# Three layers' modulation rows: from TensorE in the recurrence and attentions to GpSimd products and ScalarE row sums in projection and feed-forward

## The reference, cut to what matters

```
# first block (a bidirectional gated delta rule, then a convolved gated feed-forward)
mod  = silu(c)  @ w_mod[0] + b_mod[0]          # 6 x 1024; shift1, scale1 are needed at once
h    = rms(x) * (1 + scale1) + shift1;  x = x + gate1 * mixer(h)
h    = rms(x) * (1 + scale2) + shift2;  x = x + gate2 * ffn(h)
# layer 2.0 (sliding-window attention + gated linear attention), layer 2.1 (causal attention)
mod2 = silu(c_2) @ ada_w[layer] + ada_b[layer] # 6 x 1024 for each of the two layers
...  x = x + gate1 * mixer(h);  x = x + gate2 * mixture_of_experts(h)
```

## Time and profile before

| what | value |
|---|---|
| median of three runs (lowest, highest) | 2882.66 us (2880.57, 2885.34) |
| the profiled execution, first to last instruction (its span) | 2876.6 us, 6.1 below the median |
| mean granted TensorE clock | 0.970 of full speed |
| `gdn_project` | 41.4 to 320 us; a round from round 2 to 3 takes 14.1 us |
| `gdn_prepare`, `gdn_core` | 320 to 334.7, 334.7 to 739.9 us |
| `gdn_finish` | 739.9 to 820.6 us; TensorE's last seven tiles 766 to 815 |
| `ffn` | 820.6 to 1244.6 us; an input round 12.1 us; output tiles from 1103 |
| `even_attention` | 1378 to 1459 us |
| `causal` | 2221 to 2298.6 us |

### The profile page before, as it was taken

How to read it: one execution, slowest core, us unless ns; L and a number is a source line. 1 busy time by engine, 2 the same in 40 slices (tenths; PEclk the granted TensorE clock), 3 DMA queues, 4 the chain that set the end, 5 groups by cost and what they waited for, 6 DMA issues and landing times. The chain is left out here.

```text
span 2876.6 us, 36427 instructions
## 1 busy us (share of the span) xinstructions
PE 2668.0 (93%) x13974; PEld 1723.2 (60%) x13974; DVE 1433.5 (50%) x2832; ACT 630.3 (22%) x1348; POOL 157.4 (5%) x179
## 2 busy tenths in 40 slices
PE   6999899999999999979998699999799998899998
PEld 4888778889568888858654233333587544333332
DVE  4767566677356675466524132234554623233334
ACT  3132355556411110012332000000213421000000
POOL 0000222222000000000100000000000000000000
PEclk8999999999999999999999899999999999899999
DMA  6111555420222222222547999999422558999998
GB/s 267 59 49 69 173 171 171 147 89 16 88 73 88 87 84 86 88 68 74 191 165 280 417 418 417 418 418 418 153 79 77 159 199 337 418 417 418 417 418 353
DMA packets 112694, 613.86 MB, mean 213 GB/s; under 512 B 12976, under 2 KB 13440, under 8 KB 62720
## 3 DMA queue, kind: packets, MB, share of 16 engines
q1 hardware_dynamic: 102240, 576.68, 52.2%
q0 software_dynamic: 8832, 30.44, 3.0%
q10 hardware_dynamic: 1440, 4.29, 0.4%
HBM read 602.85 MB, written 8.51 MB: 213 GB/s over the span
## 5 line engine op out<-in xcount | busy, mean ns | idle before, releaser
L3099 PE MATMUL bank<-arena 128*32 128x512 f32 (+2 forms) x2048 | 407.0, 613 | 39.2 <-DMA arena<-in_w 30.9
L470 PE MATMUL bank<-arena 128*128 128x256 f32 x1776 | 409.7, 384 | 20.3 <-ACT arena L438 13.9
L470 PEld LDWEIGHTS bank<-arena 128*128 128x128 f32 x1776 | 338.3, 192 | 88.8 <-issue 33.7
L3099 PEld LDWEIGHTS bank<-arena 128*32 128x32 f32 (+2 forms) x2048 | 137.7, 132 | 284.8 <-issue 279.1
L3127 PE MATMUL bank<-arena 128*32 128x512 f32 (+2 forms) x1024 | 210.8, 636 | 37.1 <-DMA arena<-in_w 34.8
L3141 PE MATMUL bank<-arena 128*128 128x512 f32 x448 | 219.6, 614 | 5.5 <-DVE arena L3260 1.8
L259 PE MATMUL bank<-arena 128*128 128x512 f32 (+1 forms) x608 | 210.0, 502 | 0.9 <-PEq L2546 0.9
L3274 DVE SCALAR_TENSOR_TENSOR arena<-bank,arena 128x512 f32<-128x512 f32 x224 | 168.3, 751 | 74.0 <-PE bank L3141 62.0
L3127 PEld LDWEIGHTS bank<-arena 128*32 128x32 f32 (+2 forms) x1024 | 69.5, 136 | 173.6 <-issue 168.9
L259 PEld LDWEIGHTS bank<-arena 128*128 128x128 f32 x608 | 114.9, 189 | 92.5 <-issue 85.4
L3141 PEld LDWEIGHTS bank<-arena 128*128 128x128 f32 x448 | 71.3, 188 | 151.7 <-DVE arena L3274 90.0
(11 more groups left out here) (492 smaller groups left out, 3957.2 us busy)
## 6 DMA issues: line engine op xcount, KB each, us to landing
arena<-in_w SPq DMA_DIRECT2D x384, 1024.0 KB, 20.1
arena<-in_dense SPq DMA_DIRECT2D x308, 512.0 KB, 4.3
arena<-core_rows POOLq DMA_DIRECT2D x48, 256.0 KB, 5.6
arena<-in_xT SPq DMA_DIRECT2D x2, 2048.0 KB, 12.5
token_rows<-arena ACTq DMA_DIRECT2D x8, 512.0 KB, 5.4
gdn_gate<-arena POOLq DMA_DIRECT2D x8, 256.0 KB, 2.7
arena<-gdn_gate SPq DMA_DIRECT2D x1, 2048.0 KB, 7.8
arena<-band_bias POOLq DMA_DIRECT2D x2, 1024.0 KB, 6.1
```

What stands on the lines that cost most here:

```text
L470: mm = pe.matmul(out, w[:, k, :], x[:, k, :], start=(k == 0), stop=(k == K1 - 1))
L3099: mm = pe.matmul(self.bank[2 + t][part, :], xT[i % 2][:, 2 * q + k, part], w[j][:, k, t, :], start=(q == 0 and k == 0), stop=(q == 3 and k ...
```

## The change

The 128 weight columns' tiles are no longer in `dense`. They are in an input of their own, `mods`, laid out with the output column on partitions and the 1024 weights along the row. A result is then a sum along the row of weight times condition. GpSimd multiplies a tile in place by the row `silu(c)` (for n below 32) or `silu(c_2)`, which stands on all partitions (`mod_scale`), ScalarE copies the tile onto itself and accumulates into the one column `mod_all[:, 16+n]` (`mod_sum`), and then, where told, waits for that sum and issues the load of a later tile into the slot. VectorE adds the bias for many columns at once. 32 tiles are handled in `gdn_project`, 20 in `gdn_finish`, 76 in `ffn`; three, eight, eight and four slots serve them. Nothing is left in `gdn_core`, `even_attention` and `causal`. The second condition row is activated once and stored in DRAM (`c2_dram`), and read back twice.

```diff
+    def mod_load(self, eng, n):
+        eng.dma_start(self.mod_slot(n), self.ins["mods"][n]).then_inc(self.mod_loaded[self.mod_place(n)[1]], 16)
+    def mod_scale(self, pool, n):
+        pool.wait_ge(self.mod_loaded[self.mod_place(n)[1]], 16 * self.mod_nth[n])
+        pool.tensor_tensor(self.mod_slot(n), self.mod_slot(n), self.mod_row(n), ALU.mult).then_inc(self.mod_scaled, 1)
+    def mod_sum(self, act, n, more=None):
+        act.wait_ge(self.mod_scaled, n + 1)
+        act.activation(self.mod_slot(n), self.mod_slot(n), ACT.Copy, accum_out=self.mod_all[:, 16 + n:17 + n]).then_inc(self.mod_summed, 1)
+        if more is not None:
+            act.wait_ge(self.mod_summed, n + 1)
+            self.mod_load(act, more)
...
 # gdn_project, ScalarE
+                def mods(i, q):
+                    n = 4 * (i - 1) + q
+                    if 0 <= n < 32:
+                        self.mod_sum(act, n, n + 3 if n + 3 < 32 else None)
+                act.dma_start(c_row, self.ins["c_rows"][0]).then_inc(self.mod_row_loaded, 16)
+                act.dma_start(c2_row, self.ins["c_rows"][1]).then_inc(self.mod_row_loaded, 16)
+                self.mod_load(act, 1)
+                self.mod_load(act, 2)
                 self.shift_steps(act, jobs, scaled, ready)
+                act.wait_ge(self.mod_row_loaded, 32)
+                act.activation(c2_row, c2_row, ACT.Silu).then_inc(c_silu, 1)
+                act.activation(c_row, c_row, ACT.Silu).then_inc(c_silu, 1)
+                act.wait_ge(c_silu, 1)
+                act.dma_start(self.c2_dram[:, :], c2_row).then_inc(c2_stored, 16)
                 for i in range(12):
+                    mods(i, 0)
+                    if i == 0:
+                        act.wait_ge(c2_stored, 16)
+                        self.mod_load(act, 0)
...
 # gdn_core, TensorE
-                    if p < groups:
-                        pieces += [(mod_rows, k, 0) for k in range(sum(steps[:l]), sum(steps[:l + 1]))]
...
 # gdn_finish
                 sp.dma_start(gate, self.gate_dram.rearrange("p (h t) -> p h t", h=H)).then_inc(gate_in, 16)
+                sp.dma_start(self.mod_row(32), self.c2_dram[:, :]).then_inc(self.mod_row_loaded, 16)
+                for n in range(32, 40):
+                    self.mod_load(sp, n)
...
+                def mods(m):
+                    for n in range(32 + 3 * m, min(35 + 3 * m, 52)):
+                        self.mod_sum(act, n, n + 8)
...
 # ffn: GpSimd, ScalarE's input loop, ScalarE's output loop, VectorE's end
+            @block.gpsimd
+            def _(pool):
+                for n in range(52, 100):
+                    self.mod_scale(pool, n)
+                pool.wait_ge(self.mod_row_loaded, 64)
+                for n in range(100, NMODS):
+                    self.mod_scale(pool, n)
...
+                    if m < J + 1:
+                        for n in range(52 + 4 * m, 56 + 4 * m):
+                            self.mod_sum(act, n, n + 8 if n + 8 < 100 else None)
...
+                for n in range(100, 104):
+                    self.mod_load(act, n)
                 for k in range(KD):
+                    if k % 2 == 0:
+                        for n in range(100 + 7 * k // 2, 107 + 7 * k // 2):
+                            self.mod_sum(act, n, n + 4 if n + 4 < NMODS else None)
...
+                self.mod_keep(dve, 32, NMODS)
```

More of the change, by code:

```diff
@@ L271, in row_product @@
         return mm
[L274 to L293, removed]
-                                 bank[:, 256:264].rearrange("p (n q) -> p q n", q=4),
-                                 self.S("mod_b", at, at + 8).rearrange("p (q n) -> p q n", q=4), ALU.add)
+    def mod_place(self, n):
+        part = max((p for p in MOD_FIRST if MOD_FIRST[p] <= n), key=MOD_FIRST.get)
+        first = MOD_FIRST["finish" if part == "ffn_in" else part]
+        return part, (n - first) % MOD_SLOTS[part]
@@ L861, in _ @@
                 last.then_inc(zeroed, 1)
+                pool.wait_ge(c_silu, 2)
+                for n in range(32):
+                    self.mod_scale(pool, n)
                 for h in range(H):
@@ L1127, in _ @@
                     for u in range(2):
-                        if u == 1 and p < groups:
-                            mod_turn(p)
                         pe.wait_ge(s["r"], 2 * p + u + 1)
@@ L1197, in _ @@
                                 act.activation(buf[u]["zs"], Z[u], ACT.Copy).then_inc(s["zts"], 1)
-                        if l == 6 and p < groups:
-                            act.wait_ge(self.w_done, w0 + KD * (p + 1) + KD)
-                            act.wait_ge(s["modm"], p + 1)
-                            act.activation(rows, self.bank[7][:, 0:256], ACT.Copy).then_inc(s["modk"], 1)
                         for u in range(2):
@@ L1473, in residual_squares @@
             act.activation(self.norm_acc if m == 0 else self.norm_sq[m % 2], self.x[:, m, :], ACT.Square).then_inc(squared, 1)
+            if beside is not None:
+                beside(m)
         act.wait_ge(total, 1)
@@ L2330, in linear_chunk @@
                     mm.then_inc(g["u"], 1)
-                def mod_steps(n, ks):
-                    for k in ks:
-                        if k == 0 and n >= 1:
-                            pe.wait_ge(m["added"], n)
-                        self.mod_tile(pe, "mod_even", n, k, self.bank[7])
                 scores(0, 0)
@@ L2350, in _ @@
                     linear_chunk(n, 0)
-                    mod_steps(n, range(6, 8))
                     turn(n, 2)
@@ L2454, in _ @@
                     state(n, 1)
-                    dve.wait_ge(m["turned"], n + 1)
-                    self.mod_keep(dve, part, n, self.bank[7]).then_inc(m["added"], 1)
             @block.scalar
@@ L2538, in causal @@
         far = self.cols(free + 2600, 8)
-        mod_rows, part, w0 = self.cols(free + 4672, 256), "mod_odd", TILE0["mod_odd"]
-        mod_kept, mod_out, mod_added = (self.sem("odd_mod_" + n) for n in ["kept", "turned", "added"])
-        SPAN = 10
         def width(n):
@@ L2621, in _ @@
                         scale(j - 1)
-                    if j % SPAN == 0 and 1 <= j // SPAN <= UNITS["mod_odd"]:
-                        dve.wait_ge(mod_out, j // SPAN)
-                        self.mod_keep(dve, part, j // SPAN - 1, self.bank[7]).then_inc(mod_added, 1)
                 scale(N - 1)
```

143 lines of the change are left out of this document (65 added, 78 removed).

## The result

The changed kernel takes 2918.2 us (2917.2 to 2919.1), the kernel before 2883.3 on the same chip: 1.2% slower, ratio 1.012 (95% interval 1.010 to 1.014). The prediction was 2845, 1.3% faster. The profiled execution of the changed kernel has a span of 2915.9 us against 2876.6.

The account below looks back on a forecast made before the run. TensorE's order was taken to set the time; 59.1 us of gain less 21.1 of cost gave -38.0, from the 2882.7 median to 2844.7 us. Its own range was 2834 to 2856 (chance 0.60), the wider range 2828 to 2868.

Parts of the forecast that it names:

- projection: First projection, 32 GpSimd products in rounds 1 to 8: cost 7 us, bounds 0.7 and 15.
- The price of a product: All 128 added GpSimd products of 128x1024: 1.90 us each, taken from the only rows of that shape.
- start: Start of the feed-forward: eight products fall among VectorE's two-operand SBUF operations, 13.1 us cost, bounds 0 and 15.2.
- rounds: Feed-forward loop, twelve rounds with four products each: mostly hidden in VectorE's waits and bank reads, 1 us cost in all.
- output tiles: Tail of the feed-forward: 28 products have 120 us, nothing is late, cost 0.
- Where products fall: Feed-forward loop: products run 4.3 us after their loads are issued, mostly while VectorE waits or reads banks; 1 us cost.
- The bound of 33 us: Feed-forward loop: if all four products of a round hit VectorE, 2.8 us a round, 33 us.
- Rival (c): Slower than before: products and VectorE's operations alternate in every round, 83 us cost against 59, 2907 us; chance 0.07.
- The price of a meeting: Where VectorE has a two-operand SBUF operation waiting: a 1.90 us product costs it about 1.64, 0.28 less than its length.
- Recurrence: 72 tiles removed from TensorE: 4.41 us in each of eight groups, plus 2 for the first unit, 37.3 us gain.
- First attention: 32 tiles removed from TensorE: eight pairs in the chain and a turn count, 9.5 us gain, bounds 5 and 18.
- Second attention: 24 tiles removed from TensorE at 0.45 us each, plus stalls of the units: 12.3 us gain, bounds 8 and 17.

Follow-up runs that it names:

- eight-value run: Changed kernel with each GpSimd product's second operand replaced by eight values, each repeated 128 times, modulations left out of the result: 2873.2 us, ratio to before 0.997.
- gated run: Changed kernel with the feed-forward's GpSimd products held until VectorE has finished its sums and is about to wait itself: 2861.3 us, ratio to before 0.992.
- half products: Changed kernel with each GpSimd product of 128x1024 made as two of 128x512: 2894.1 us, ratio to before 1.0036.

## Why the prediction was wrong

The sign was wrong. The forecast added 21.1 us of cost to 59.1 of gain; in the profiles the cost is 80 (10.9 in the projection, 20.3, 27.3 and 21.2 in the feed-forward) and the gain 38 by the stages, 40 by the run without any modulation work. Two steps of the cost failed, the price of one product and the places where products fall, and one of the gain.

*The price of a product.* "1.90 us each by the only rows of that shape" took the shape for the whole story. That row's second operand is four values, each repeated 256 times; a product of two full rows takes 2.34 undisturbed. With 1.89 three of the forecast's terms are nearly met: start 15.2 above before (forecast 13.1), rounds 2.8 (forecast 1), projection 9.8 (forecast 7). The fourth is not: the output tiles lose 9.4 (forecast 0). With 2.34 they are 20.3, 27.3, 10.9 and 21.2. The price alone is worth the 45 us of the eight-value run. Even there, with the 1.89 that the forecast took, the time is 28 us above the forecast. (The Trainium skill, "GPSIMD Engine Reference", section "Elementwise — side-by-side cycle accounting", gives 4.50 us for a two-operand fp32 addition of 2048 elements, since both operands come through one port; half of it, 2.25 as an estimate, is near the 2.34 measured.)

*Where products fall.* "4.3 us later the products run: mostly while VectorE waits or reads banks", so 1 us in the loop and 0 at the output tiles. They came in rows of eight and of eleven. In the changed kernel ScalarE's sums of two rounds follow each other closely (891.7 to 898 and 900 to 906 us), so that eight loads are issued in 13 us and eight products run without a gap; that a round lengthened by products is what brings the sums of two rounds together is read from the order of the rows, and no run isolated it. The bound of 33 us held for the loop (27.3 measured), though it left out that a third of the loss would be TensorE's lower clock behind its waits. At the output tiles the forecast gave no bound above 0, and 21.2 was measured: "28 products have 120 us" counted the time and not when the loads land. The gated run shows that the timing was the cause: 8 and 0 remain. Rival (c), the alternation of products and VectorE's operations, was the right mechanism and had 0.07. That its 2907 is near 2918 is partly luck: it took the hits as spread over twelve and eight rounds, priced the projection at 27 and a gate at 10 that cost 10.9 and 0, gave the output tiles nothing where 21.2 was lost, and had 59 as the gain.

*The price of a meeting.* This step held. The forecast put it at 0.28 less than GpSimd's length: the scalings, 0.61 apart before, are 2.75 apart now, that is 2.14 more beside a product of 2.34, or 0.20 less. That the later one waits for nearly all of the other is thus what the trace shows, except where one is shut out for longer.

*What removal gives.* Forecast 59; the stages give 28.5 + 13.3 - 3.9 = 38, and the run without any modulation work 40 in all.
- Recurrence 37.3 forecast, 28.5 measured. By the marks of L1323, only three periods gave the 4.4 of the forecast (35.4 to 31.0). The four before them, which "should also lose 4.4", gave 3.0, 3.0, 2.3 and 3.1; the stretch up to the first mark gave 3.3, where 4.4 and 2 for the first unit were forecast, and the period behind the three 0.4. In the early groups VectorE's L1306 comes next and takes 1.41 us instead of 0.69 beside GpSimd; from group 5 on it is 0.69. The 2.3 holds 0.7 of lower clock.
- First attention 9.5 forecast, with bounds 5 to 18; it lost 3.9. "I am wrong if TensorE's granted clock falls where its filling is gone" stood in the text without a price; it fell from 0.94 to 0.80, and with it kept up the stage gives 5.7 against before.
- Second attention 12.3 forecast, 13.3 measured. The granted clock did not fall there: 0.96 before, 0.97 now.

Right were the gated output projection at 0 (80.8 both times, with 20 products in it), and that bytes, sums and issues cost nothing.

## What to carry to other kernels

Work on GpSimd is free only while VectorE does not run instructions that read two operands from SBUF. Price it by the VectorE operations that it will meet, each of them longer by nearly a whole GpSimd instruction however short it is itself, and let GpSimd wait for a semaphore that VectorE sets just before it waits or reads banks; left to the arrival of loads, the products bunch, and even a stage with far more time than work can lose by it, as the output tiles lost 21 us. Take the duration of an added instruction from a row with the same operands, not only the same output shape. And before filler is taken out of a waiting TensorE, or a wait is added to it, ask what the clock does: idle products in the wait took 9.6 us off the stage and 8 off the whole.

## What the runs showed of the hardware

- Two full operands cost GpSimd 2.34 us for 128x1024, one full and one of four or eight repeated values 1.89; VectorE takes 1.22 for two full ones.
- VectorE and GpSimd usually take turns, one instruction each, with a joint period of 2.75 us (product 2.34, scaling 0.61 alone). With half products one VectorE addition was shut out for 26.8 us over 21 of GpSimd's. What decides between the two was not found.
- VectorE's operations of 128x256 with one operand in a bank keep their 0.42 us beside GpSimd's products, in all runs that have them.
- Behind waits of TensorE of 3.1 to 5.5 us in the feed-forward its granted clock was 0.5 to 0.6 for some 3 to 4 us, and 24 product records took 7.15 to 8.44 us instead of 5.36.
- The same projection code took between 290.5 and 299.9 us in the profiles of five programs, for a reason not found; the recurrence, where nothing was added, stayed between 376.6 and 378.1 us.
